# Expert loop over whole experts, with six ring slots of 22 to 24 KB

## The reference, cut to what matters

```python
N_EXPERTS, EXPERT_FF, EC_CAPACITY_FACTOR = 16, 2816, 2
def expert_choice_moe(h, w_router, w_gate, w_up, w_down):
    B, L, D = h.shape
    cap = max(1, EC_CAPACITY_FACTOR * L // N_EXPERTS)
    aff = jax.nn.softmax(jnp.einsum('bld,de->ble', h, w_router).astype(jnp.float32), axis=-1)
    gate, idx = lax.top_k(jnp.swapaxes(aff, 1, 2), cap)
    xs = jax.vmap(lambda hb, ib: hb[ib])(h, idx)
    hid = jax.nn.silu(jnp.einsum('becd,edf->becf', xs, w_gate)) * jnp.einsum('becd,edf->becf', xs, w_up)
    out = jnp.einsum('becf,efd->becd', hid, w_down) * gate[..., None].astype(h.dtype)
    return jax.vmap(lambda ob, ib: jnp.zeros((L, D), ob.dtype).at[ib.reshape(-1)].add(ob.reshape(-1, D)))(out, idx)
```

## Time and profile before

| | |
|---|---|
| median of three runs | 1985.57 us (1985.0 to 1986.83) |
| profiled execution | 1986.42 us |
| its span | 1984.6 us |
| PE busy | 1910.4 us (96%) |
| DVE busy | 1207.5 us (61%) |
| ACT, POOL busy | 395.4 us, 394.6 us (20% each) |
| weights queue (q1) | 134,576 packets, 617.71 MB, 77.5% of 16 engines |
| instruction fetches of PE (q8) | 42 packets, 0.69 MB, 0.1% |
| DMA rate | mean 326 GB/s; 405 to 420 GB/s in the slices of the loop |
| chain that ended last | PE 76%, DMA 12%, DVE 4%, SPq 3%, issue 3% |

### The profile page before, as it was taken

One profiled execution on the slowest core, in us unless ns is written; L12 is line 12 of the kernel. 1 busy time (PEld: TensorE's weight loads), 2 busy tenths in 40 slices (PEclk: granted clock), 3 DMA queues, 4 the chain that ended last, 5 costly groups with the idle time before them and its releaser, 6 DMA issues.

```text
span 1984.6 us, 64364 instructions
## 1 busy us (share of the span) xinstructions
PE 1910.4 (96%) x28594; PEld 1604.4 (81%) x28594; DVE 1207.5 (61%) x1969; ACT 395.4 (20%) x909; POOL 394.6 (20%) x406
## 2 busy tenths in 40 slices
PE   8999999999997999999999999999999999999996
PEld 5888899999873888788877778779777687877874
DVE  3532441232556777687676867767677676867764
...
DMA  8244542312359999999999999999999999999997
GB/s 334 86 161 151 176 129 64 107 51 79 127 220 363 412 407 419 408 411 415 408 418 409 414 412 411 415 407 420 407 411 416 407 419 408 412 414 412 414 411 288
DMA packets 150463, 647.58 MB, mean 326 GB/s; under 512 B 11420, under 2 KB 56344, under 8 KB 134024
## 3 DMA queue, kind: packets, MB, share of 16 engines
q1 hardware_dynamic: 134576, 617.71, 77.5%
...
...
HBM read 632.47 MB, written 14.40 MB: 326 GB/s over the span
## 4 chain that ended last, share of the span: by engine, by line
PE 76%; DMA 12%; DVE 4%; SPq 3%; issue 3%; ACT 1%; POOL 0%; POOLq 0%; DVEq 0%; ACTq 0%
PE bank L2386 17%; PE bank L2414 16%; PE bank L1985 16%; PE bank L2403 9%; DMA ring<-in_w_exp_gate_dram 9%; PE bank L2396 6%; PE bank L2106 3%; PE bank L2252 2%; SPq L568 2%; DMA ring<-in_w_exp_down_dram 1%; PE bank L2311 1%; SPq L575 1%; PE bank L1956 1%; PE bank L1967 1%; DMA x_in<-in_x_sample_dram 1%
## 5 line engine op out<-in xcount | busy, mean ns | idle before, releaser
L1715 DVE TENSOR_TENSOR sums<-ring 128x704 f32<-128x704 f32 x744 | 608.5, 886 | 191.8 <-PE bank L2403 168.2
L2386 PE MATMUL bank<-ring,hid_t 128*32 128x256 f32 x8184 | 480.4, 379 | 12.9 <-DVE hid_t L1787 7.2
L2414 PE MATMUL bank<-ring,xs_t 128*32 128x352 f32 x5952 | 453.1, 459 | 0.0
L2386 PEld LDWEIGHTS bank<-ring,hid_t 128*32 128x32 f32 x8184 | 380.6, 110 | 79.4 <-issue 9.8
L2414 PEld LDWEIGHTS bank<-ring,xs_t 128*32 128x32 f32 x5952 | 307.5, 110 | 128.3 <-issue 7.6
L2403 PE MATMUL bank<-sums,xu_a 128*32 128x176 f32 x5952 | 296.5, 313 | 18.3 <-issue 17.8
L2403 PEld LDWEIGHTS bank<-sums,xu_a 128*32 128x32 f32 x5952 | 241.9, 110 | 42.6 <-issue 40.3
L791 POOL TENSOR_TENSOR small<-kpow 128x2 f32<-128x2 f32 x31 | 10.4, 334 | 993.1 <-DVE out_rows L1846 868.1
L1167 ACT ACTIVATE v_both<-bank 128x176 f32<-128x176 f32 x31 | 9.9, 318 | 856.0 <-PE bank L2403 856.0
L2396 PE MATMUL bank<-ring,xu_a 128*32 128x176 f32 x1984 | 173.8, 313 | 0.0
L1985 PE MATMUL bank<-act_hi,wt_hi 128*128 128x320 f32 x448 | 138.8, 310 | 0.8 <-DVE rtmp L1526 0.8
...
## 6 DMA issues: line engine op xcount, KB each, us to landing
ring<-in_w_exp_gate_dram SPq DMA_DIRECT2D x128, 1408.0 KB
ring<-in_w_exp_up_dram SPq DMA_DIRECT2D x128, 1408.0 KB
...
```

Of the source, the lines that this page charges most:

```text
L1715: nc.vector.tensor_tensor(sums[:, (N_SUM * i + j) % SUM_SLOTS], w[:, k, :, n, :], w[:, kk, :, nn, :], ALU.add if sign > 0 else ALU.subtrac ...
L2386: ins = mm(bank[5 + x // 2][c * Q:(c + 1) * Q, x % 2 * DC:(x % 2 + 1) * DC], hid_t[:, f, x * Q:(x + 1) * Q], w[:, j, c * DC:(c + 1) * DC], ...
L2414: ins = mm(bank[UP_BANK[x]][c * Q:(c + 1) * Q, 0:FC], xs_t[:, x, k * Q:(k + 1) * Q], w[:, kk, c * FC:(c + 1) * FC], start=k == 0, stop=k = ...
```

## The change

One step now is one whole expert, and every engine's loop has an expert as its body. Expert 0 is done whole before the loop, and the loop runs over the other 15 (its down pieces are those of the expert before).

- *Pieces.* A gate or up piece is two whole weight rows per partition, 22,528 bytes in one run. Down pieces are 6, 5, 5 and 6 rows of 4096 bytes (24,576 or 20,480). There are still four of each kind, in the order g0 d0 g1 d1 g2 d2 g3 d3 u0 to u3: g3 and d3 have changed places.
- *Ring.* Six slots of 22 to 24 KB (`SLOT_AT`) hold them, for twelve of 12 KB. One more buffer (`extra`, over the place of `sums`) holds one piece of expert 0.
- *Sums.* A sum is 1408 elements per partition, and there are four slots for sums of it (704 and eight). DVE now waits for `sum_used`, which PE raises after each unit that used a sum, before it writes a slot again. PE waits for each sum by itself. The units have another order (`UNITS`): R11, R22, V2, V1, R21, V4, V3, V5, V6, R12.
- *Banks.* A unit is 352 columns per column group. With the down products in two banks, the units V1 to V4 are split over two or three banks (`PLACES`), so some matmuls are 64, 96, 128, 160, 192 or 256 columns wide. ACT copies all gate products out of the banks (14 copies, and seven more that prepare the combination; before there were ten per half), and `combine` works on the copies.
- *DVE's order.* `combine` stands ahead of the scaled down rows; the old kernel has them the other way round. The two halves of down rows need no addition any more. `hidden` is split: the two sample tiles come ahead of sums V5 and V6 of the next g0, and the prompt tile behind them. `down` waits for the three tiles of `hid_t` one at a time.
- *End.* The last down pieces are five (5, 6, 5, 4, 2 rows), the rows of the accumulator are fetched before they are consumed, and the last rows are added to them directly.

```diff
-FTH = FF // P // 2
-FH = FF // 2
...
-RING = 12
-STEPS = 2 * NE
-FIRST = 8
+RING, STEP_N, FIRST = 6, 12, 8
+SPARE_AT = 4
...
-PIECE = 3 * D
-DOWN_AT, DOWN_N = (0, 3, 6, 9), (3, 3, 3, 2)
...
-STEP = (("g", 0), ("d", 0), ("g", 1), ("d", 1), ("g", 2), ("d", 2), ("d", 3), ("g", 3), ("u", 0), ("u", 1), ("u", 2), ("u", 3))
+DOWN_AT, DOWN_N = (0, 6, 11, 16), (6, 5, 5, 6)
+LAST_AT, LAST_N = (0, 5, 11, 16, 20), (5, 6, 5, 4, 2)
+STEP = (("g", 0), ("d", 0), ("g", 1), ("d", 1), ("g", 2), ("d", 2), ("g", 3), ("d", 3), ("u", 0), ("u", 1), ("u", 2), ("u", 3))
...
+N_SUM, SUM_SLOTS = 6, 4
 SUMS = ((1, 0, 0, 0, -1), (0, 1, 1, 1, -1), (1, 0, 1, 1, 1), (0, 0, 0, 1, 1), (0, 0, 1, 1, 1), (0, 1, 1, 0, 1))
...
-SUM_AT = ((2, 0), (2, FN), (3, 0), (3, FN), (4, 0), (4, 0))
-OWN_AT = ((R11, 0, 0, 0, 0), (R22, 0, FN, 1, 1), (R21, 1, 0, 1, 0), (R12, 1, FN, 0, 1))
-AHEAD = 6
+OWN = {R11: (0, 0), R22: (1, 1), R21: (1, 0), R12: (0, 1)}
+UNITS = (R11, R22, V2, V1, R21, V4, V3, V5, V6, R12)
+PLACES = {R11: ((3, 0, 0, 352),), R22: ((4, 0, 0, 352),), R21: ((7, 0, 0, 352),), R12: ((0, 0, 0, 352),),
+          V5: ((1, 0, 0, 352),), V6: ((1, 0, 0, 352),),
+          V2: ((2, 0, 0, 192), (3, 352, 192, 160)), V1: ((2, 192, 0, 192), (4, 352, 192, 160)),
+          V4: ((2, 384, 0, 128), (0, 352, 128, 160), (7, 352, 288, 64)), V3: ((6, 256, 0, 256), (7, 416, 256, 96))}
...
+UP_AT = (((0, 0, 0, 352), (1, 0, 352, 352)), ((2, 0, 0, 352), (7, 0, 352, 352)), ((5, 0, 0, 512), (6, 0, 512, 192)))
...
-                sp.wait_ge(e_used, s + 1)
-                src = (w_exp_gate, w_exp_up)[up][0, ahead:NE][expert_at(e)].rearrange("a (p k) f -> p (a k) f", k=KT)\
-                    [:, 2 * i:2 * i + 2, (1 - half) * FH:(2 - half) * FH]
-                sp.dma_start(ring[slot][:, 0:2 * FH].rearrange("p (k f) -> p k f", f=FH), src).then_inc(e_landed[slot], 16)
...
+                src = (w_exp_gate if kind == "g" else w_exp_up)[0, ahead:NE][expert_at(e)]\
+                    .rearrange("a (p k) f -> p (a k f)", k=KT)[:, 2 * i * FF:(2 * i + 2) * FF]
+                sp.dma_start(dst[:, 0:2 * FF], src).then_inc(landed, 16)
...
+            def piece(n, t, e, ahead):
+                slot = slot_of(t)
+                sp.wait_ge(e_used, n)
...
+            with sp.Fori(0, NE - 2) as e:
+                for t in range(3, STEP_N):
+                    piece(STEP_N * e + FIRST + t + 1, t, e, 0)
+                for t in range(3):
+                    piece(STEP_N * e + STEP_N + FIRST + t + 1, t, e, 1)
...
+                for u, n in ((V3, 0), (R12, 0), (V4, 1), (V5, 0), (V2, 0), (V1, 0), (V4, 0), (R21, 0), (V4, 2), (V3, 1),
+                             (R11, 0), (R22, 0), (V2, 1), (V1, 1)):
+                    b, o, f, w = PLACES[u][n]
+                    nc.scalar.activation(cols[u][:, f:f + w], bank[b][:, o:o + w], ACT.Copy).then_inc(e_evict, 1)
...
                 for j in range(first, last):
+                    q = N_SUM * i + j
+                    if q >= SUM_SLOTS or not isinstance(r, int):
+                        dve.wait_ge(sum_used, 4 * N_SUM * r + q - SUM_SLOTS + 1)
                     k, n, kk, nn, sign = SUMS[j]
-                    nc.vector.tensor_tensor(sums[:, (N_SUM * i + j) % SUM_SLOTS], w[:, k, :, n, :], w[:, kk, :, nn, :],
+                    nc.vector.tensor_tensor(sums[:, q % SUM_SLOTS], w[:, k, :, n, :], w[:, kk, :, nn, :],
                                             ALU.add if sign > 0 else ALU.subtract).then_inc(sums_done, 1)
...
+                nc.vector.transpose(hid_t[:, :, x * Q:(x + 1) * Q],
...
+                if ahead:
+                    nc.vector.tensor_copy(idx_gather[:].unsqueeze(1), idx_all[:, 2:NE, :][:, expert_at(r), :]).then_inc(e_idx, 1)
+                for i in range(1, KT // 2):
+                    piece_sums(r, i, 0, N_SUM)
+                dve.wait_ge(e_used, STEP_N * r + RING + FIRST + POS["g", 3] + 1)
+                combine(r)
+                rows(r)
+                if ahead:
+                    rows_ahead(r + 2)
+                    piece_sums(r + 1, 0, 0, SUM_SLOTS)
+                hidden_samples(r)
+                if ahead:
+                    piece_sums(r + 1, 0, SUM_SLOTS, N_SUM)
+                hidden_prompt(r)
...
+                    if i == 0:
+                        pe.wait_ge(e_hid, NX * r + x + 1)
+                    if i == 3 and x == 2:
+                        pe.wait_ge(e_evict, EVICT * r + 1)
...
-                for j in range(N_SUM):
-                    b, o = SUM_AT[j]
-                    if j % 2 == 0:
-                        pe.wait_ge(sums_done, 4 * N_SUM * r + N_SUM * i + j + 2)
-                    for c in range(4):
-                        ins = mm(bank[b][c * Q:(c + 1) * Q, o:o + FN], unit(j)[:, i, :], sums[:, (N_SUM * i + j) % SUM_SLOTS, c, :],
...
+                for u in UNITS:
+                    if i == 0 and u == V2:
...
+                    if u < N_SUM:
+                        pe.wait_ge(sums_done, 4 * N_SUM * r + N_SUM * i + u + 1)
+                    for b, o, f, wide in PLACES[u]:
+                        for c in range(4):
+                            if u < N_SUM:
+                                src = sums[:, (N_SUM * i + u) % SUM_SLOTS, c, f:f + wide]
+                            else:
+                                src = w[:, OWN[u][0], c, OWN[u][1], f:f + wide]
+                            ins = mm(bank[b][c * Q:(c + 1) * Q, o:o + wide], unit(u)[:, i, :], src,
+                                     start=i == 0 and (u, b) in OPENS, stop=i == KT // 2 - 1, skip_group_check=True)
+                    if u < N_SUM:
+                        ins.then_inc(sum_used, 1)
                 ins.then_inc(e_used, 1)
...
+                w = ring[slot][:, 0:2 * FF].rearrange("p (k f) -> p k f", f=FF)
+                for x in range(NX):
+                    if i == 0:
+                        if x < 2:
+                            pe.wait_ge(e_evict, EVICT * r + (4, 10)[x])
+                        else:
...
+                        for b, o, f, wide in UP_AT[x]:
+                            for c in range(4):
...
-            with pe.Fori(0, STEPS - 1) as r:
...
+            with pe.Fori(0, NE - 1) as r:
+                for t in range(STEP_N):
...
-                    if (kind, i) == ("d", 0):
-                        pe.wait_ge(e_hid, NX * r + NX)
...
+                    pe.wait_ge(e_landed[slot], 32 * r + 16 * landing(t))
```

573 lines of the change are left out of this document (278 added, 295 removed).

## The result

The changed kernel takes 2122.39 us (median of 4 runs, 2120.85 to 2124.59) where the kernel before takes 1986.2 us (4 runs, 1985.0 to 1989.23). The ratio is 1.0684, with a 95% interval of 1.0666 to 1.0703: 6.8% slower. I had forecast 2060 us and a range of 2000 to 2090. The direction was right and the size was not: the time lies outside the range by 32 us. The profiled execution took 2120.85 us, with a span of 2119.0 us against the 2058.7 of the sum.

The account below looks back on a forecast made before the run. PE (84.3 us per expert) and DMA (85.5) were taken as near-equal limits. New PE passes of 86.9 us, with start, tail and 42 us of code fetches, summed to 2058.7, forecast as 2060 us (3.7% slower), range 2000 to 2090.

Parts of the forecast that it names:

- the sum: Whole program: 666.5 before the loop, 5.7 once, 15 passes of 86.9, 41.0 tail, 42 for code: 2058.7 us.
- the stutter: During POOL's last gather per expert, PE gets only a few matmuls at a time: 3.5 us per expert, kept unchanged.
- The instruction queue: Sign at the code fetch queue: present through the whole loop, with some 11 packets per expert.
- the price of a fetch: At PE's loop branch: 3.0 us standing for one code block, 14 times, 42 us, from 25 to 52.
- The waits for V6: In each of four gate pieces PE waits 0.56 us for DVE's late sum: 2.2 us per expert.
- The wait for the banks: PE's up phase waits until DVE has read the down rows: 0.2 us per pass, 1.2 if copies are slower.
- The narrow matmuls: PE's matmuls of 64 and 96 columns: 0.2 us per expert taken, between nothing and about 1.3.
- the loop began: Before the loop, expert 0 is done whole, 45.0 us of PE products from 621.47; loop start forecast at 666.5 us.
- the tail: After the loop: last down matmuls 28.9 us, plus waits and the ending, in all 41.0 us (before 31.4).
- Rival B: At PE's loop branch: code stays held or comes early enough, all else as forecast: 2018 us, chance 0.22.
- two limits 1.5% apart: Old expert loop: PE sets 84.3 us per expert early, DMA 85.5 later, so changing DMA alone wins little.
- Larger runs per partition: Gate and up loads in 22.5 KB runs: DMA gains at least 0, at most 2% (1.7 us) from 85.5 us.

Follow-up runs that it names:

- a_best: Changed kernel with PE's expert loop written out, V6 behind three quarters of R12, and the first pass's sums V5 and V6 made earlier: 2014.81 us.
- b_fill: Kernel before with four unused 352-column additions on DVE behind the two sums of g2 in the even step, beside the last gathers: 1986.29 us, ratio 0.9999.
- a_fill: Changed kernel, PE loop written out, V6 later, first sums early, plus three unused 512-column DVE additions between g1's fourth and fifth sums: 1990.15 us, ratio 1.0017.

## Why the prediction was right and wrong

**Right: which way, and by what.** The body of PE's loop went from 1572 to 2822 instructions by my count, and the branch fetches its target. In the traces a pass has 1576 and 2826 records of PE, so the count was good. Most of the loss is this branch: a_best, with the stutter in its passes and no branch, is at 2014.81 us, and 108 of the 136 us are gone (5 of them by its shorter first g0). The written-out loop alone is at 1993.49 because the stutter went too. The instruction queue stays busy through the loop as said (13 packets per expert, where I had 11; the written-out loop has 11, so the other two come with the branch).

**Wrong: the price of a fetch, the first term of the sum that failed.** I took 3.0 us, between two small DMAs of 1.8 and 3.7, and kept 52 us as the upper bound for 14 of them. It is 5.3 us, above both rows. One block's packet takes 1.07 us, but PE stands for five times that: some 2.1 us until the packet starts, 1.0 for it, and 2.0 behind it. The rows were small DMAs of another kind in another stretch, so they bounded nothing; an honest upper bound would have been wider.

**Missing: the clock, a term that the sum put at nothing.** I priced the stall as lost time alone. PE comes out of it at a granted clock of 0.50, and g0 takes 2.6 us longer. Nothing in the old loop showed this, as PE never stood still for that long there. But the old trace shows it ahead of the loop: PE stands for 9.2 us until 615.6, and the granted clock is 0.50 from 612 to 620.

**The other terms, per pass.** The sum said 86.9 + 3.0 = 89.9 us and 93.9 were measured. The stall adds 2.3 and the half clock 2.6. The waits for V6 were forecast at 2.2; there are three, of 0.53 to 0.6 us, and the fourth lies under the half clock, so 0.6 less. The stutter is 2.9 for 3.5. The wait for the banks, for which I took 0.2 and named 1.2, is 0.8. The narrow matmuls cost nothing (g2 is 5.9 and one wait), 0.2 less. In sum 89.9 + 2.3 + 2.6 - 0.6 - 0.6 + 0.6 - 0.2 = 94.0.

The pass shown is a little longer than most. The 13 between the first and the last take 93.6 us on average, 3.7 above the sum, which is 48 of the 60 us between the spans. The rest: the loop began at 673.5 and not 666.5, since the first expert's rows came 4 us later and its products took 47.8 us for 45.0. The first pass took 100.7 us for 95.6, and the tail 42.7 for 41.0. Against these, the last pass has no gathers and no stutter, and took 1.7 us less than forecast.

**Rival B, no fetch, was priced at 2018 us.** The written-out loop gives 1993.49, and a_best, whose passes are those of rival B with the stutter in (86.64 us, forecast 86.9), gives 2014.81. The 21 us between them are the stutter, which I had taken as fixed to the gathers. It isn't: it needs them, but work on DVE beside them removes it, and small edits elsewhere switched it on or off.

**What bounds the kernel before.** I read 84.3 us early and 85.5 late, and called them two limits 1.5% apart. b_fill shows that the lower one did not count for the time of the program: the ring runs ahead by only half an expert, and what PE wins early it gives back.

**Larger runs per partition.** With 22.5 KB runs the loop of a_fill moved 418 GB/s from 740 to 1330 us where the kernel before moved 412, and 412 against 413 after that. Some 3.3 MB of the whole traffic are code. So the range of 0 to 2% was right. Where the gain went (the code, a smaller lead at the start, the longer tail) no run separates. No version of whole experts beat the kernel before; the nearest is 0.17% slower.
